# A three-block transformer forward pass on one core: the last two normalisations applied behind the products instead of ahead of them

## The reference, cut to what matters

```python
def rms_norm(x, gain):
    y = x * rsqrt(mean(x * x, axis=-1, keepdims=True) + EPS)
    return y * gain

def mixer_sublayer(x, norm_g, w_in, b_f, q_gain, k_gain, out_gain, w_out):
    proj = rms_norm(x, norm_g) @ w_in            # 1024 x (3*1024 + 6 + 384)
    q, k, v = ...                                # 16 heads of 64
    f_logit = proj[..., 3072:3078] + b_f         # 6 forget gates
    g_fox = proj[..., 3078:]                     # 384 output-gate columns
    q = rms_norm(q, q_gain); k = rms_norm(k, k_gain)   # per head
    ... # three kinds of causal attention, each normalised, one times sigmoid(g_fox)
    return x + concat(...) @ w_out

def mlp_sublayer(x, norm_g, w_up, w_down):       # w_up: 1024 x 4096
    return x + square(relu(rms_norm(x, norm_g) @ w_up)) @ w_down
```

## Time and profile before

| | |
|---|---|
| median of three runs | 2615.6 us (2613.13, 2615.6, 2626.5) |
| the profiled execution | 2615.97 us; its span is 2614.2 us |
| PE busy | 2461.7 us, 94% of the span |
| weight loads (PEld) | 1931.5 us, 74% |
| DVE, ACT, POOL busy | 983.0, 861.1, 773.3 us (38%, 33%, 30%) |
| chain that ended last, by engine | PE 81%, issue 6%, DVE 4%, DMA 3%, POOL 3%, ACT 2% |

### The profile page before, as it was taken

One profiled execution on the slowest core, in us unless ns is written; L12 is line 12 of the kernel. 1 busy time (PEld: TensorE's weight loads), 2 busy tenths in 40 slices (PEclk: granted clock), 3 DMA queues, 4 the chain that ended last, 5 costly groups with the idle time before them and its releaser, 6 DMA issues.

```text
span 2614.2 us, 34014 instructions
## 1 busy us (share of the span) xinstructions
PE 2461.7 (94%) x13345; PEld 1931.5 (74%) x13345; DVE 983.0 (38%) x1420; ACT 861.1 (33%) x1397; POOL 773.3 (30%) x413
## 2 busy tenths in 40 slices
PE   6998999899999999799999889999899998899998
PEld 3676667688888887588577668888677756688887
DVE  4356641411111112444457242222365263523433
ACT  3234642321112122332556232222343463323321
POOL 1151002122222222231011334444443531344443
PEclk8999999899999999899999989999999998899999
DMA  7550007222222115321010223333323201233332
GB/s 255 169 161 25 2 13 225 78 59 62 65 64 64 58 58 177 90 73 43 7 42 2 69 69 97 97 97 95 99 73 81 78 2 33 72 97 96 93 97 78
DMA packets 335970, 209.76 MB, mean 80 GB/s; under 512 B 29299, under 2 KB 308444, under 8 KB 335842
## 3 DMA queue, kind: packets, MB, share of 16 engines
q1 hardware_dynamic: 332880, 201.89, 26.3%
q10 hardware_dynamic: 2898, 6.05, 0.6%
q0 software_dynamic: 64, 0.04, 0.0%
HBM read 205.82 MB, written 2.12 MB: 80 GB/s over the span
## 4 chain that ended last, share of the span: by engine, by line
PE 81%; issue 6%; DVE 4%; DMA 3%; POOL 3%; ACT 2%; SPq 0%; DVEq 0%; POOLq 0%; ACTq 0%
PE G L1514 20%; PE G L1515 20%; PE G L1516 20%; PE G L1678 5%; PE G L1691 4%; PE G L1706 4%; POOL wlo L868 3%; DMA raw<-in_l_ada_w_dram 2%; PE G L1581 1%; PE G L1649 1%; PE G L1548 1%; PE G L1532 1%; PE G L1724 1%; PE G L1533 1%; PE G L1534 1%
## 5 line engine op out<-in xcount | busy, mean ns | idle before, releaser
L868 POOL TENSOR_TENSOR wlo<-raw,whi 128x1024 fp32r<-128x1024 f32 x282 | 680.6, 2414 | 1605.0 <-ACT whi L1054 1605.0
L1514 PE MATMUL G<-big_a,whi 128*128 128x512 f32 x1984 | 729.5, 368 | 15.0 <-POOL wlo L868 12.2
L1515 PE MATMUL G<-big_a,wlo 128*128 128x512 f32 x1984 | 716.3, 361 | 0.0
L1516 PE MATMUL G<-big_a,whi 128*128 128x512 f32 x1984 | 712.6, 359 | 0.0
L1054 ACT ACTIVATE whi<-raw 128x1024 fp32r<-128x1024 f32 x282 | 298.8, 1060 | 1237.1 <-PE G L1516 1034.5
L1514 PEld LDWEIGHTS G<-big_a,whi 128*128 128x128 f32 x1984 | 374.3, 189 | 91.3 <-POOL wlo L868 15.3
L1515 PEld LDWEIGHTS G<-big_a,wlo 128*128 128x128 f32 x1984 | 374.2, 189 | 61.9 <-issue 6.5
L1516 PEld LDWEIGHTS G<-big_a,whi 128*128 128x128 f32 x1984 | 373.3, 188 | 59.1
L1514 PE MATMUL G<-big_b,whi 128*128 128x512 f32 x856 | 316.6, 370 | 7.3 <-DVE big_b L2333 3.5
L1515 PE MATMUL G<-big_b,wlo 128*128 128x512 f32 x856 | 315.7, 369 | 0.0
L1516 PE MATMUL G<-big_b,whi 128*128 128x512 f32 x856 | 314.3, 367 | 0.0
(11 more groups left out here) (232 smaller groups left out, 2361.7 us busy)
## 6 DMA issues: line engine op xcount, KB each, us to landing
raw<-in_l_ada_w_dram SPq DMA_DIRECT2D x96, 512.0 KB, 5.0
raw<-in_l_ffn_w_gate_dram SPq DMA_DIRECT2D x44, 512.0 KB, 3.8
raw<-in_l_ffn_w_up_dram SPq DMA_DIRECT2D x44, 512.0 KB, 3.8
raw<-in_l_ffn_w_down_dram SPq DMA_DIRECT2D x32, 512.0 KB, 4.1
raw<-in_w_up_dram SPq DMA_DIRECT2D x32, 512.0 KB, 4.0
raw<-in_w_down_dram SPq DMA_DIRECT2D x32, 512.0 KB, 3.7
raw<-in_w_in_dram SPq DMA_DIRECT2D x28, 512.0 KB, 3.8
raw<-in_l_w_in_dram SPq DMA_DIRECT2D x24, 512.0 KB, 3.9
```

The costliest lines, as they stand in the source:

```text
L868: pool.tensor_tensor(wlo[:, u % 2], raw[:, r % RING], whi[:, u % 2].bitcast(F32), ALU.subtract).then_inc(raw_free[r % RING], 1)
L1514: pe.matmul(o, whi[:, u % 2, k], rlo[:, k, t0:t0 + w], start=k == 0, stop=False)
L1515: pe.matmul(o, wlo[:, u % 2, k], rhi[:, k, t0:t0 + w], start=False, stop=False)
L1516: mm = pe.matmul(o, whi[:, u % 2, k], rhi[:, k, t0:t0 + w], start=False, stop=k == k_tiles - 1)
```

## The change

The gain is multiplied into the residual tile and the tile is split as soon as it is ready, inside the loop before the norm; the factor 1/rms is applied when a product is read out of PSUM. Its sum, root and spreading are issued inside the second unit behind the norm. In the input projection the value units come first, then queries, keys, forget and output gates. In the last feed-forward DVE applies relu and 1/rms in one instruction and ACT squares twice. The rounding of the first two output units' weights moves into the local attention's loop. In the diff below, the lines that it leaves unchanged are cut out, and the headings after @@ name the part:

```diff
+        invb, invt = ssq[:, 0:TX], stat[:, 2, 0:16]
@@ planner
+                if n == 1 and deferred is not None:
+                    plan_aux(("spread", deferred), plan_aux(("norm", deferred)))
...
-        B2_COLS = [[(128 * i, 128)] for i in range(25)] + [[(3078 + 128 * i, 128)] for i in range(3)]
+        B2_COLS = [[(128 * (16 + i), 128)] for i in range(8)] + [[(128 * i, 128)] for i in range(16)]
+        B2_COLS += [[(3 * D, 128)]] + [[(3078 + 128 * i, 128)] for i in range(3)]
...
+        plan_aux(("spread", 5), plan_aux(("norm", 5), plan["up", 2, 0, 3][2]))
+        DEFERRED = {4: "an2", 5: "mn2"}
@@ ScalarE
             def residual_square(i, m, n):
...
+                if i in DEFERRED:
+                    act.activation(hhi[:, m, 0:n], xT[:, m, 0:n], ACT.Copy,
+                                   scale=vc(DEFERRED[i], m)).then_inc(PH[f"norm{i}", "hi"], 1)
                 act.activation(sq[:, m % 2, 0:n], xT[:, m, 0:n], ACT.Square).then_inc(PH[f"res{i}", "sq"], 1)
+            def deferred_root(i):
+                act.wait_ge(*auxiliary(("norm", i)))
+                act.activation(invt[:, 0:4], ps(("norm", i), 4), ACT.Sqrt,
+                               bias=eps[:, 0:1]).then_inc(PH[f"norm{i}", "std"], 1)
...
+                        if n in sums and deferred is not None:
+                            s, w = sums[n]["s"], sums[n]["n"]
+                            act.wait_ge(*when((st, "evac"), s + 1))
...
+                            act.activation(sq[:, s % 2, 0:w], qr[:, s % 2, 0:w],
+                                           ACT.Square).then_inc(PH[st, "square"], 1)
@@ local attention, ScalarE
+                    if n in (9, 11):
+                        upper(plan["wout", 1, (n - 9) // 2][0])
...
-            upper(plan["wout", 1, 0][0])
-            upper(plan["wout", 1, 1][0])
@@ last feed-forward, ScalarE
+                    def plain_squares(b, j):
+                        t = tiles + b
+                        act.wait_ge(*when((sems, "act"), t + 1 + 4 * j))
...
+                        act.activation(sq[:, b % 2, 0:n], qr[:, b % 2, 0:n], ACT.Square).then_inc(PH[sems, "prod"], 1)
+                        act.activation(ahi[:, bass.ds(j * 4 + b, 1), 0:n] if not isinstance(j, int)
+                                       else ahi[:, b + 4 * j:b + 4 * j + 1, 0:n],
+                                       qr[:, b % 2:b % 2 + 1, 0:n], ACT.Square).then_inc(PH[sems, "hi"], 1)
@@ output gates
-                    release(act.activation(gsig[:, i, :], ps(key, TX), ACT.Sigmoid), key)
+                    act.wait_ge(*when(("in2", "evac"), 18 + i))
+                    act.activation(gsig[:, i, :], gsig[:, i, :], ACT.Sigmoid).then_inc(PH["in2", "gate"], 1)
@@ TensorE
+            def mean_squares(i):
+                a, g = plan["norm", i]
+                pe.wait_ge(*when((f"res{i}", "ssq"), KD))
+                take_group(g)
+                for t in range(4):
+                    mm = pe.matmul(G[g % 4][:, t:t + 1], ssq[:, P * t:P * t + P], ones_d[:, 0:1], start=True, stop=True)
+                aux(mm)
+            def spread_roots(i):
+                a, g = plan["spread", i]
+                pe.wait_ge(*when((f"norm{i}", "diag"), 1))
+                aux(pe.matmul(G[g % 4][:, 0:TX], ones_d, rsb[:, 0, 0:TX], start=True, stop=True))
+            def late_norm(i):
+                return {2: lambda: mean_squares(i), KD - 1: lambda: spread_roots(i)}
...
+                    if c == 0 and l == 2:
+                        unit(("up", l, 0, 0), hhi, hlo, ranges, h_ready=h_ready)
+                        unit(("up", l, 0, 1), hhi, hlo, ranges, between=late_norm(5))
+                        unit(("up", l, 0, 2), hhi, hlo, ranges)
+                        pe.wait_ge(*when(("norm5", "inv"), 1))
+                        unit(("up", l, 0, 3), hhi, hlo, ranges)
@@ VectorE
+            def deferred_norm(i):
+                dve.wait_ge(*when((f"norm{i}", "std"), 1))
+                link(dve.reciprocal(invt[:, 8:12], invt[:, 0:4]))
+                dve.scalar_tensor_tensor(out=rsb[:, 0, 0:TX].rearrange("p (a b) -> p a b", b=P),
+                                         in0=ident.rearrange("p (a b) -> p a b", a=1).broadcast_to([P, 4, P]),
+                                         scalar=float(D),
+                                         in1=invt[:, 8:12].rearrange("p (a b) -> p a b", b=1).broadcast_to([P, 4, P]),
+                                         op0=ALU.mult, op1=ALU.mult).then_inc(PH[f"norm{i}", "diag"], 1)
+                dve.wait_ge(*auxiliary(("spread", i)))
+                return dve.tensor_copy(invb, ps(("spread", i), TX))
...
+                    if m >= 1 and i in DEFERRED:
+                        dve.wait_ge(*when((f"norm{i}", "hi"), m))
+                        dve.scalar_tensor_tensor(out=hlo[:, m - 1, 0:n], in0=xT[:, m - 1, 0:n], scalar=vc(DEFERRED[i], m - 1),
+                                                 in1=hhi[:, m - 1, 0:n].bitcast(F32), op0=ALU.mult,
+                                                 op1=ALU.subtract).then_inc(PH[f"norm{i}", "h"], 1)
                     if m >= 1 and i is not None:
                         sum_squares(i, m - 1, n)
...
-                            dve.tensor_tensor(sq[:, b % 2, 0:n], qr[:, b % 2, 0:n], qr[:, b % 2, 0:n],
-                                              ALU.mult).then_inc(PH[sems, "prod"], 1)
+                            dve.scalar_tensor_tensor(out=qr[:, b % 2, 0:n], in0=G[g][:, 0:n], scalar=0.0, in1=invb,
+                                                     op0=ALU.max, op1=ALU.mult).then_inc(PH[sems, "act"], 1)
...
+                release(dve.tensor_tensor(v2[:, :, P * i:P * i + P], ps(key, TX).rearrange("p (a b) -> p a b", a=4),
+                                          invt[:, 8:12].rearrange("p (a b) -> p a b", b=1).broadcast_to([P, 4, P]),
+                                          ALU.mult), key)
...
+            def scaled_unit(n):
+                key = ("in2", "U", n)
...
+                dve.wait_ge(*product_of(key))
+                dve.tensor_tensor(dst, ps(key, TX, rows), invb[0:rows], ALU.mult).then_inc(PH["in2", "evac"], 1)
```

More of the change, by code:

```diff
@@ L322, in plan_norm, with plan_inputs @@
             plan_aux(("spread", n))
-        def plan_inputs(st, units, vts, sums, two=(), ada=()):
+        def plan_inputs(st, units, vts, sums, two=(), ada=(), deferred=None):
             seq = []
@@ L1099, in inputs @@
                 for n in range(n_units + 1):
+                    if n == 1 and deferred is not None:
+                        deferred_root(deferred)
                     if n < n_units:
@@ L1326, in plain_turn @@
                     def plain_turn(j):
+                        first = c == 0 and isinstance(j, int) and j == 0
+                        if first:
+                            next_weights(0, j)
+                            deferred_root(5)
                         for b in range(4):
-                            act.wait_ge(unit_done, u0 + b + 1 + 4 * j)
-                            upper(u0 + b + 2, j)
-                            t = tiles + b
-                            if t >= 2 or not isinstance(j, int):
-                                act.wait_ge(*when((sems, "lo"), t - 1 + 4 * j))
@@ L1470, in forget @@
                 link2(act.activation(lsig[0:N_FOX, :], lsig[0:N_FOX, :], ACT.Ln, bias=1.0))
-                free(act, key)
             fcount = [0]
@@ L1491, in _ @@
             wout(2, 5, TX)
-            norm(5, X_ONLY, lambda k, q: zero8[:, k:k + 1])
             ffn(2, FF2_CHUNKS, X_ONLY, None)
@@ L1501, in take_group, with unit @@
                     pe.wait_ge(gfree[g % 4], g // 4)
-            def unit(key, rhi, rlo, ranges, k_tiles=KD, j=0, h_ready=None):
+            def unit(key, rhi, rlo, ranges, k_tiles=KD, j=0, h_ready=None, between={}):
                 u, r, g = plan[key]
@@ L1628, in inputs @@
                     if op == "U":
-                        if n == 0:
+                        if deferred is not None and n < 2:
+                            unit((st, "U", n), rhs[0], rhs[1], ranges_of(n), h_ready=h_ready if n == 0 else None,
+                                 between=late_norm(deferred) if n else {})
+                        elif n == 0:
                             first_units([(st, "U", 0), (st, "U", 1)], ranges_of, h_ready)
@@ L1883, in _ @@
             ffn(1, FFN_CHUNKS, X_ONLY, ("norm3", "h"))
-            norm(4, TX)
-            inputs("in2", S2, tuple(range(16, 24)), (hhi, hlo), 28, lambda n: X_ONLY, h_ready=("norm4", "h"))
+            inputs("in2", S2, tuple(range(8)), (hhi, hlo), 28, lambda n: X_ONLY, h_ready=("norm4", "h"), deferred=4)
             pe.wait_ge(*when(("in2", "normed"), 16))
```

81 lines of the change are left out of this document (51 added, 30 removed).

## The result

The changed kernel takes 2576.4 us (median of 4 runs, 2576.0 to 2578.8) against 2616.1 (4 runs); the ratio is 0.984, with an interval of 0.982 to 0.985: 39.8 us faster. The profiled execution has a span of 2574.2 us. The forecast was 2575.

The account below looks back on a forecast made before the run. PE, busy 94% of the span, was taken as the bound, so gains come only where it waits or its clock falls. Gains of 40.7 from 2615.97 gave 2575.3, as median 2575 us; range 2569 to 2582, with rivals 2567 to 2588.

Parts of the forecast that it names:

- norm 4: Behind the down product: two units and the norm end at 1895.0 instead of 1909.5; gain 14.5 us (13 to 15.6).
- norm 5: Third unit starts at 2246.4 instead of 2261.58, with 0.8 of stall; gain 15.2 us (13.5 to 16).
- output product of layer 2: Behind the attention: start 6.45 us sooner, 2.3 from the clock, less 0.75 for moved work; gain 8.0 (5 to 8.8).
- last feed-forward: Four waits of PE, 3.5 us in all, where down products follow up units, go; gain 3.5 (2 to 3.5).
- input projection: Query and key units cost 0, 0.5 us of stall at the last unit; together -0.5 (-2 to +1).
- The root's chain: Norm 4: root, reciprocal and diagonal matrix, some 1.5 us, hide behind 15 matmuls (3.4 us); slack about 2 us.
- that rival: The clock falls at the new sums: 11 matmuls lose 2.3 us and the sum 0.9, at two places; +6.5, 2582; 7%.
- The down loop: Ahead of norm 4: one more `hlo` (0.75 us) per down unit on VectorE; taken as 0, up to 5 in all.
- the same chain: Norm 5's stall comes from norm 4's `hlo` chain, with GpSimd's subtraction sooner over; 0.8 us (0 to 2.4).
- Only VectorE's own 4.8 must fit: Input projection: units overlap through two-deep buffers, so only VectorE's 4.8 us must fit into PE's 6.3; cost 0.
- the chain closes on itself: Input projection, slower side: each of 16 units takes 9.5 us against 6.3, 51 in all, giving 2626; 3%.

Follow-up runs that it names:

- experiment 3: Changed kernel with the one-column sums of norms 4 and 5 issued ahead of the first unit instead of inside the second; 2591.9 us, ratio 0.989.
- experiment 1: Changed kernel with the two weight roundings put back behind the local attention; 2583.8 us, ratio 0.986.
- experiment 5: Kernel before with only the last feed-forward's chain changed, with ones for 1/rms and norm 5 still ahead of the products; ratio 0.998.
- experiment 7: Experiment 6 plus the forget gates' running sums one unit earlier in VectorE's list, behind the evacuation of unit 25 instead of 26; 2568.8 us, ratio 0.981.
- experiment 4: Changed kernel with VectorE doing the evacuation of each of the 16 query and key units twice; 2584.9 us, ratio 0.987.
- experiment 8: Changed kernel again without an edit, as base on the same chip and second profile; 2581.4 us, ratio 0.985.
- experiment 6: Changed kernel with the first two units of the last two output products one behind the other instead of interleaved tile by tile; 2566.3 us, ratio 0.981.
- experiment 9: Changed kernel with the input projection's units in the old order (queries, keys, values, gates), late norm kept; ratio 0.984.

## Why the prediction was right, by its steps

| step | forecast | between the two profiles |
|---|---|---|
| norm 4 | 14.5 | 14.6 |
| norm 5 | 15.2 | 15.7, of which 0.3 belong below |
| output product of layer 2 | 8.0 | 6.5 + 2.4 - 0.7 = 8.2 |
| last feed-forward | 3.5 | 4.9 - 0.3 (from norm 5) = 4.6 |
| input projection | - 0.5 | - 0.45 |
| all that is unchanged | 0 | - 2.6 |
| sum | 40.7 | 40.0 |

- **Norm 4** is right in its parts too: 13.75 us for two units and the norm, 13.8 forecast. Two stops with a slower start behind them cost 1.0 (1.1 forecast), the sum 0.9 at full clock, the spreading 0.85. The root's chain stayed hidden. Experiment 3 shows that the place of the sum carried it, and that the clock did fall as soon as TensorE waited there: that rival was about the place, and its price was 1.87 for the sum and 12 slow products.
- **The down loop** cost 0.1 on TensorE, 0 forecast and within its spread over the profiles, for the reason given: GpSimd started first and ran its 2.40, and VectorE waited.
- **Norm 5** gained 0.5 more: only one stop was left (0.7, forecast 0.8), and from the spreading's start to the third unit's it was 0.46 us instead of 0.95. But the third unit's first product then took 0.80 and its next one came 0.64 later, 0.3 more than before the change; this 0.3 falls into the last feed-forward in the table, and 15.4 is the fair figure. That "the same chain" as at norm 4 gives the stop was wrong: the addition took the collision, not `hlo`.
- **The output product:** 6.46 of wait (6.45 forecast) and 2.43 of clock (2.3). The clock's part is luck of this pair of profiles. The forecast expected the clock to stay through the gap ahead of the first product, and in six of nine profiles with early rounding it did not (experiment 1). On average over ten profiles the clock gave 1.3, and 7 is the better figure for the whole step.
- **The last feed-forward** was mis-sized: the listed idle time was taken as the price of a stop. It is 1.21 for a listed 0.88 (experiment 5).
- **The input projection** came out at the forecast size, but not by the forecast's sum. Three things make up the - 0.45. The last unit has its stop for GpSimd's weights, 0.3 with the slower first product (0.5 forecast):

```profile
2044.08 0.39 PE L1546 MATMUL G<-big_a,whi 128*128 128x512 f32 x1
2044.50 0.50 PE L1544 MATMUL G<-big_a,whi 128*128 128x512 f32 x1
```

  One slower start behind a head sum more falls into this stretch, 0.3, which the forecast did not have. And the idle time ahead of the attention is 1.79 instead of 1.98; it would be 0.93 if the scan did not meet GpSimd's subtraction (experiment 7), which the forecast did not have either. "Only VectorE's own 4.8 must fit" failed: the loop over two engines had 0.22 us to spare, not 1.5 (experiment 4). The rival of the slower side ("the chain closes on itself") asked the right question with a wrong sum: the loop took 6.1 a unit, not 9.5, since the rounding and GpSimd's subtraction are not in it. But it would have begun to cost with 0.3 us more, and the 3% given to it rested on a margin that wasn't there.
- **The unchanged part** moved by - 3.1 ahead of the change and + 0.5 around the attention, which is chance (experiment 8). In this pair it hid that the steps together gave some 2 us more than forecast; with 7 for the output product they give about 1 us more. That 40.7 and 40.0 agree so well is therefore partly luck, where each step is right within about 1 us.

What stays open: why the clock fell behind a stop of 3 us, or behind the start with 0.89 us of idle time, in some executions and not in others. No run isolates it.

## What to carry to other kernels

A per-row factor that can be applied behind a product frees the product from the whole chain of its norm; put the sum and the spreading inside running products, because there they also cost half and leave the clock up. Before adding an instruction to an engine with much idle time, follow the loop in which its results return to it: gaps under 0.1 us between its members mean that the loop, not the busy share, is the limit, as in experiment 4. A stop costs more than its listed idle time, here 1.21 for 0.88, and some 2.5 us more where 12 products behind it run at half clock. So weights prepared in time are worth more than the wait that the profile lists for them: 4.4 and 4.9 us on average for waits of 2.98 and 2.99 (experiment 6).

## What the runs showed of the hardware

- A scan on 6 partitions with SBUF operands took 3.30 us when it started behind a GpSimd subtraction and 1.21 when it started ahead of one; that subtraction then took 3.03 (experiment 7).
- The same eight one-column matmuls took 1.87 us behind a stop of 6.07 and 0.95 between products (experiment 3).
- Behind stops of 3 us the granted clock stayed at 1.00 in one execution and was 0.50 for the next 5 us in another of the same kernel (experiment 6). Behind a stop of 2.17 us 7 products ran at half clock (experiment 9), and in six of nine profiles 7 or 8 behind the end of the local attention, with 0.89 us of idle time ahead of them (experiment 1).

The fastest version found is that of experiment 6, 2566.3 us; that of experiment 7, 2568.8 us, is not told apart from it.
